# Nine whole u_tab chunks ahead of the one-hot rounds instead of ten, seven spread among the rounds, and the last tokens' transposes moved in between

## What is computed

```python
best, ci = lax.top_k(cand, PEER_TOPK)
e1 = jnp.take_along_axis(i1, ci // PEER_TOPK, axis=-1)
e2 = jnp.take_along_axis(i2, ci % PEER_TOPK, axis=-1)
expert = (e1 * N_KEYS + e2).reshape(T, PEER_HEADS * PEER_TOPK)
gate = jax.nn.softmax(best, axis=-1).reshape(T, PEER_HEADS * PEER_TOPK).astype(h.dtype)
...
u = jnp.take(u_tab, ec, axis=0)
act = jax.nn.gelu(jnp.einsum('cd,ckd->ck', hc, u), approximate=False) * gc
vv = jnp.take(v_tab, ec, axis=0)
return jnp.einsum('ck,ckd->cd', act, vv)
```

## Time and profile before

| | us |
|---|---|
| median of 3 runs | 3491.82 (3491.78 to 3492.76) |
| profiled execution, time | 3488.36 |
| profiled execution, span of the trace | 3486.6 |
| TensorE clock granted, mean over the span | 0.986 |
| PE busy | 3322.8 (95%) |
| DVE busy | 2565.2 (74%) |
| ACT busy | 1586.2 (45%) |

### The profile page before, as it was taken

The page is one execution under the profiler, slowest core; times in us unless marked ns, Lnnn a source line. Parts: engine busy times, 40 slices in busy tenths (PEclk is TensorE's granted clock), DMA queues, the critical chain, the costliest instruction groups (busy, mean ns, idle before and its releaser), DMA issues.

```text
span 3486.6 us, 68596 instructions
## 1 busy us (share of the span) xinstructions
PE 3322.8 (95%) x24838; PEld 2971.3 (85%) x24838; DVE 2565.2 (74%) x4511; ACT 1586.2 (45%) x2501; POOL 115.6 (3%) x122
## 2 busy tenths in 40 slices
PE   7999999999999899988888899999999999999998
PEld 6888788888888787777777799899999999999998
DVE  6766587776868778766665688877777777777776
ACT  5445454444444455433333422454444545454543
POOL 0000000000000000000000001100000000101000
PEclk9999999999999999999999999999999999999999
DMA  5544545555555544430002445677778787878764
GB/s 194 176 135 164 174 151 169 197 167 194 176 193 183 174 138 143 141 102 10 8 21 92 169 157 177 235 273 269 274 262 286 275 306 270 301 253 303 249 233 157
DMA packets 175005, 658.30 MB, mean 189 GB/s; under 512 B 19745, under 2 KB 28065, under 8 KB 165281
## 3 DMA queue, kind: packets, MB, share of 16 engines
q1 hardware_dynamic: 159744, 559.15, 47.9%
q0 software_dynamic: 15104, 97.03, 7.8%
HBM read 637.99 MB, written 17.04 MB: 188 GB/s over the span
## 4 chain that ended last, share of the span: by engine, by line
PE 81%; DVE 9%; DMA 4%; ACT 3%; issue 2%; ACTq 0%; SPq 0%; DVEq 0%
PE bank L612 45%; PE bank L614 22%; PE bank L950 5%; DVE w_lo L1992 3%; PE bank L1246 3%; DMA raw<-in_v_tab 2%; ACT w_hi L1331 2%; PE bank L1286 1%; DMA raw<-in_u_tab 1%; DVE proj L2550 1%; PE bank L635 1%; PE bank L921 0%; PE bank L895 0%; DVE stage L2002 0%; DMA gates<-g_stage 0%
## 5 line engine op out<-in xcount | busy, mean ns | idle before, releaser
L612 PE MATMUL bank<-h_two,w_hi 128*128 128x512 f32 (+1 forms) x5360 | 1824.0, 391 | 51.4 <-DVE h_two L2050 20.5
L614 PE MATMUL bank<-h_two,w_lo 128*128 128x256 f32 (+1 forms) x5360 | 1467.8, 274 | 0.0
L1992 DVE TENSOR_TENSOR w_lo<-raw,w_hi 128x1024 fp32r<-128x1024 f32 (+1 forms) x1054 | 1228.1, 1184 | 237.8 <-ACT w_hi L1331 235.0
L1331 ACT ACTIVATE w_hi<-raw 128x1024 fp32r<-128x1024 f32 (+1 forms) x1054 | 1045.8, 1024 | 496.6 <-PE bank L614 291.2
L612 PEld LDWEIGHTS bank<-h_two,w_hi 128*128 128x128 f32 x5360 | 1009.3, 188 | 238.8 <-issue 42.8
L614 PEld LDWEIGHTS bank<-h_two,w_lo 128*128 128x128 f32 x5360 | 1019.3, 190 | 1.1 <-issue 0.7
L612 PE MATMUL bank<-p_two,w_hi 128*128 128x448 f32 x1792 | 573.8, 378 | 15.2 <-DVE acc L2017 15.2
L614 PE MATMUL bank<-p_two,w_lo 128*128 128x224 f32 x1792 | 478.0, 267 | 0.0
L612 PEld LDWEIGHTS bank<-p_two,w_hi 128*128 128x128 f32 x1792 | 338.7, 189 | 48.9 <-DVE w_lo L1992 17.1
L614 PEld LDWEIGHTS bank<-p_two,w_lo 128*128 128x128 f32 x1792 | 344.6, 192 | 0.0
L1336 ACT ACTIVATE stage<-bank 128x256 f32<-128x256 f32 (+1 forms) x242 | 89.4, 369 | 401.3 <-PE bank L614 401.2
(11 more groups left out here) (402 smaller groups left out, 3264.4 us busy)
## 6 DMA issues: line engine op xcount, KB each, us to landing
raw<-in_u_tab SPq DMA_DIRECT2D x256, 512.0 KB
raw<-in_v_tab SPq DMA_DIRECT2D x256, 512.0 KB
raw<-in_w_up SPq DMA_DIRECT2D x176, 512.0 KB
raw<-in_w_in SPq DMA_DIRECT2D x174, 512.0 KB
raw<-in_w_out SPq DMA_DIRECT2D x64, 512.0 KB
raw<-in_w_down SPq DMA_DIRECT2D x64, 512.0 KB
raw<-in_w_pq SPq DMA_DIRECT2D x32, 512.0 KB
gates<-g_stage POOLq DMA_DIRECT2D x14, 896.0 KB, 6.3
```

The costliest lines, as they stand in the source:

```text
L612: nc.tensor.matmul(o[:, 0:2 * width].rearrange("p (a t) -> p a t", a=2), wh, pair[:, :, 0:width], start=(k == 0), stop=False)
L614: last = nc.tensor.matmul(o[:, width:2 * width], wl, pair[:, 0, 0:width], start=False, stop=(k == nk - 1))
L1331: nc.scalar.activation(w_hi[c % 2][:, at:end], raw[c % 2][:, at:end], ACT.Copy).then_inc(hi_done, 1)
L1992: nc.vector.tensor_tensor(w_lo[c % 2][:, at:end], raw[c % 2][:, at:end], w_hi[c % 2][:, at:end].bitcast(F32), ALU.subtract).then_inc(lo_do ...
```

## The change

`EARLY` goes from 10 to 9. The seven whole chunks that remain, 112 tiles, are dealt out over the first 48 rounds by 2, 2 and 3 (`WHOLE_BY`); a Gelu follows in the round in which its chunk ends (6, 13, 20, 27, 34, 41, 47). The four parts of `by_token` follow rounds 10, 14, 18 and 22, on PE and on ACT. POOL copies `h_tok` after store 6. `SPLIT_AT` goes from (40, 51) to (46, 52), `LOWER_AT` from (44, 55) to (48, 54). Since the slots' copies are now the first two of the semaphore `turned_copied`, waits on it change their numbers.

```diff
-        EARLY, EARLY_EXP = 10, 7
+        EARLY, EARLY_EXP = 9, 7
...
-        SPLIT_AT, LOWER_AT = (40, 51), (44, 55)
+        WHOLE_BY = [min(n * (DT - EARLY) // 3, DT * (DT - EARLY)) for n in range(TD // 4 + 1)]
+        WHOLE_AT = [next(n for n in range(TD // 4) if WHOLE_BY[n + 1] >= DT * (x + 1)) for x in range(DT - EARLY)]
+        TOKENS_AT = (10, 14, 18, 22)
+        SPLIT_AT, LOWER_AT = (46, 52), (48, 54)
...
                 if part >= 2:
-                    pe.wait_ge(turned_copied, part - 1)
+                    pe.wait_ge(turned_copied, part + 1)
...
-                if x in (3, 5):
-                    by_token(x - 3)
-                    by_token(x - 2)
...
-            pe.wait_ge(turned_copied, 6)
+            def whole_tile(n):
+
+                x, k = EARLY + n // DT, n % DT
+                whole_tiles(x, k, k + 1)
+
+            pe.wait_ge(turned_copied, 2)
...
-                if n < 8 * (DT - EARLY):
-                    whole_tiles(EARLY + n // 8, 2 * (n % 8), 2 * (n % 8) + 2)
+                for tile in range(WHOLE_BY[n], WHOLE_BY[n + 1]):
+                    whole_tile(tile)
+                if n in TOKENS_AT:
+                    by_token(TOKENS_AT.index(n))
...
             def by_token_copy(part):
-                act.wait_ge(peer_turned, part + 1)
+                act.wait_ge(peer_turned, part + 3)
...
-                if x in (3, 5):
-                    by_token_copy(x - 3)
-                    by_token_copy(x - 2)
...
-            act.wait_ge(peer_turned, 5)
+            act.wait_ge(peer_turned, 1)
...
-            act.wait_ge(peer_turned, 6)
+            act.wait_ge(peer_turned, 2)
...
-                if n % 8 == 7 and n < 8 * (DT - EARLY):
-                    whole_gelu(EARLY + n // 8)
+                if n in WHOLE_AT:
+                    whole_gelu(EARLY + WHOLE_AT.index(n))
+                if n in TOKENS_AT:
+                    by_token_copy(TOKENS_AT.index(n))
...
-            pool.wait_ge(turned_copied, 4)
-            for q in range(1, KQ):
-                pool.dma_start(h_tok[TG * q:TG * (q + 1), :], h_tok[0:TG, :]).then_inc(k_swapped, 16)
...
+                if b == 6:
+                    pool.wait_ge(turned_copied, 6)
+                    for q in range(1, KQ):
+                        pool.dma_start(h_tok[TG * q:TG * (q + 1), :], h_tok[0:TG, :]).then_inc(k_swapped, 16)
...
-            dve.wait_ge(turned_copied, 6)
+            dve.wait_ge(turned_copied, 2)
```

## The result

The changed kernel took 3501.65 us (median of 13 runs, 3495.14 to 3512.96), the kernel before beside it 3491.53 (13 runs, 3483.90 to 3495.61): a ratio of 1.0033 with a 95% interval of 1.0020 to 1.0045, so 7.0 to 15.7 us slower. The forecast was 3497.3, 5.5 us slower, and the time lies 0.15 us above the end of its range. The change by the medians is 10.1 us, nearly twice the forecast; the forecast counted its own 5.5 us as too small to be told from no change, and the measured interval lies clear of no change.

A forecast was written before the change was run, and what follows sets the result against it. PE was taken to bound the kernel, with DVE setting the pace in the last eight rounds. The terms 1.45 + 1.6 + 1.2 + 1.2 = 5.45 us, added to 3491.82, gave 3497.3 us; range 3488.0 to 3501.5.

The forecast's parts named there:

- chunks to transposes: Ahead of the rounds: PE waits for DVE's gates and starts the slots' transposes at about 2128.75 instead of 2135.04.
- rounds 0 to 47: Rounds 42.7 us, 112 tiles 42.4, token parts 3.7: 88.8 us in all, PE never waiting for DVE.
- slow clock at the head: Ahead of the rounds: idling lowers PE's granted clock to 0.50, costing between 0 and 1.6 us, taken as 1.2.
- rounds 48 to 55: Last eight rounds, without tiles: DVE sets the pace, 16.2 us, plus 1.6 for store 11 and 1.2 for the clock.
- What bounds the kernel: PE is later by 0.02 us a round with two tiles; the split chunks' start moves the end one for one.
- the cover for POOL's copies and store 6: Store 6 lands before ACT's round 32: no cost; without that cover 1 to 3 us.
- The tail: Last eight rounds: PE idles ahead of rounds 49 and 55; ACT's round 52 copies wait for store 11, costing 1.6 us.
- The stall after round 42: PE's earlier stall of 1.73 us, behind ACT's wait for chunk 16's load, goes with `SPLIT_AT` at 46.
- the token parts: Four parts of token transposes among the rounds cost PE 0.93 us each, 3.7 together.
- both covers holding: Rival: store 11 lands within 8 us and the clock stays at 1.00; +1.5 us (0 to +3), chance 0.20.
- the slower one: Rival: store 11, from 11.5 us on, or a like stall decides in the last rounds; over 7 us slower, chance 0.27.
- the kept head start: Rival: DVE's 6.3 us lead carries through, or the last eight rounds take 0.89 each; 7.6 us earlier, chance 0.04.

The follow-up runs named there:

- the kernel with eight chunks in front: Changed kernel with eight whole chunks ahead of the rounds instead of nine; median 3507.55 us (8 runs), ratio to the kernel before 1.0040.
- The filler: Changed kernel with nine and six matmuls of unread results in PE's two idle stretches ahead of the rounds; median 3496.58 us, ratio to before 1.0010.
- the splits moved alone: Kernel before with only `SPLIT_AT` and `LOWER_AT` changed, to (46, 52) and (48, 54); median 3493.67 us, ratio to before 0.9997.
- both parts undone: Changed kernel with token parts back ahead of the rounds and chunk 17's split and lower part back at 51 and 55; median 3490.42 us beside 3494.01 of before.

## Why the prediction was right in its sign and too small

Step by step, the changed kernel's two traces beside the terms:

| step | predicted us | measured us |
|---|---|---|
| chunks to transposes | 60.15 | 60.14, 60.18 |
| transposes to round 0 | 3.40 | 3.92, 3.92 |
| rounds 0 to 47 | 88.85 | 92.55, 92.91 |
| slow clock at the head | 1.2 | in the two lines above |
| rounds 48 to 55 | 16.2 + 1.6 + 1.2 | 18.88, 19.18 |
| sum less before | +5.45 | +8.3, +9.0 |
| slow clock behind the stretch | nothing | 1.4, 1.4 |

**What bounds the kernel** was read rightly, and the sign followed from that. PE's idle stretch ahead of the gates was forecast at 3.5 us and was 3.71; the moved work came back in the rounds at its full length or a little more, as the kernel with eight chunks in front shows (6.4 us in the rounds for the 6.1 of one more chunk); the head start on DVE's side was worth nothing. No wait of PE stands in rounds 0 to 47, so the cover for POOL's copies and store 6 held as well.

**The tail** was right in its waits: idle 2.04 ahead of round 49 (2.2 forecast), ACT waiting 2.38 us for store 11 (1 to 3), and the chain of split, lower part and last round behind it. Store 11 took 10.5 us (10 taken):

```profile
DMA to landing us min/median/max: 4.3/5.0/10.5
```

Undoing the order of that chain gave 4.2 us back in the tail. The stall after round 42 went, as forecast. The 1.2 us for the slow clock at this end was wrong in size and in place. After the 3.75 us of idling PE worked at half clock for 4.7 us, which cost 0.84 in the last round (1.73 instead of 0.89) and 1.4 in the split chunks: 2.2 in all, above the 1.6 that was given as the end. That the sum for the last eight rounds came out (19.0 against 18.88 and 19.18) is in part luck. The clock had also fallen once more there, for 3.4 us, and rounds 50 and 51 took 3.89 us together, where they took 3.25 in the kernel in which it stayed up.

**The step that failed is the term for the clock, above all at the head.** The prediction took one slow stretch like the one of the earlier trace rows, 3.2 us of work at most, and gave it 1.2 us, with 1.6 as its end. The granted clock stayed at 0.50 from 2131.7 to 2142.0, through the transposes, through the second idle stretch, and on through nearly two whole rounds, so 1.5 us of transposes and 5.1 of rounds ran slow (5.9 in the second trace). The filler prices it at 0.46 us ahead of round 0 and 2.46 in the rounds, 2.9 together. The nearest row was one idle stretch of 3.38 us with dense work behind it, and its slow time was taken for the longest there is. It isn't: here a second idle stretch of 2.4 us stood behind the first, and at the other end one stretch of 3.75 us was enough for 4.7 us of slow work. The filler closed both gaps at the head at once, so what each of them adds isn't shown, and why the slow time was 3.4 us long in one place and 6.8 or 10.2 in others stays open.

The Trainium skill (TensorE: Matmul & The Clock Gate, Part 4: PE-mode transpose) says that transposes don't count as activity in the way that matmuls do. By it the prediction would have had 1.6 for the head, still 1.3 under the 2.9 measured. The trace agrees in so far as the clock didn't rise after the six; but no run here has matmuls in their place and the idle stretches kept, so that isn't shown.

**The second term that was too small is the token parts,** 0.93 us taken from a run of sixteen alike, 1.19 measured with a round on both sides: 1.0 us for the four. The sum also has a slip of 0.2: 112 tiles at 0.38 are 42.6 us, not 42.4.

With the two terms, 1.7 and 1.0 us more, the sum is 8.2, and the measured stretch gives 8.3 and 9.0; with the 1.4 behind it 9.7 and 10.4. Set against the start of the chunks, the split chunks began at 2244.1 in the time of the trace before (2068.60 + 175.49), above the 2239 to 2243 of the prediction. The rivals: both covers holding was wrong on both counts; the slower one, which was to come from store 11, came in size but not by its cause, since the store took 10.5 us and the clock made up the difference; the kept head start was wrong.

**What stays open.** The medians differ by 10.1 us, and the stretch with the 1.4 us behind it by 9.7 to 10.4; the interval, 7.0 to 15.7, holds both. The rest of the span, where no edit lies, read 1250.4 to 1260.8 in eleven traces and 1244.0 in a twelfth, and the whole chunks began between 2065.1 and 2074.5 after the same code. The four longest rests belong to kernels with different edits. One of them, the splits moved alone, had a rest 9 us longer than before in its trace, yet a median that can't be told from before's (0.9997, 0.9982 to 1.0012), which suggests that these differences are mostly of single executions. Whether a part of them follows the places of the splits isn't settled. The range of the forecast was also too narrow for this: it allowed 3 us for the rest either way.

## What to carry to other kernels

When two engines hand work over, place the movable work so that neither waits at the hand-over. Work can be taken away from ahead of a wait at no cost only until the engine arrives there just in time. Here nine chunks with the token parts did that, and each step beyond cost its full length, and the first of them the clock too. Where the last rounds have no tiles and PE waits for DVE in them, spread the tiles to nearly the end, but not so far that they hold back the loads of the next stage. And don't put a step that a later engine needs behind a wait on a store, nor into the rounds where its engine is the later one. Last, a slow stretch that was measured once is no upper bound for the next one: here the work done at half clock after an idle stretch was 3.2 us in one place and 4.7 to 5.9 in others.

## What the runs showed of the hardware

- Idling of 3.71 us, 1.5 us of transposes and 2.38 us more of idling went with 10.2 us at half clock, in both traces, 5.1 and 5.9 us of it under full work. After 9.75 us of idling 5.8 us of full work were slow. With the stretch of 2.58 us alone the clock stayed at 1.00. Matmuls of no use in the gaps kept it at 1.00 and made the edited stretch 3.2 us shorter.
- A short idle stretch doesn't always leave the clock alone. In the last eight rounds PE idled for 2.04 us, worked for 1.16 and idled for 0.47, and the granted clock then fell to 0.50 for 3.4 us in five traces of six that have this pattern; in the sixth, with both parts undone, it stayed at 1.00.
- A group of eight records with 32 output rows between two others costs 1.19 us where its own records take 0.93 in a row.
- The store of 896 KB that was issued together with three loads of 512 KB took 11.3 us before and 10.5 after; the other 26 stores of the two traces took 4.3 to 7.1.
